# TensorE multiplies the identity matrix into an unread bank around the transposes of the RMS norms

## The reference

```
def rmsnorm(x, g):                       # first block; the second adds shift and scale
    y = x * rsqrt(mean(x * x, axis=-1) + 1e-6)
    return y * g
first block, for l in 0, 1:
    h = rmsnorm(x, norm_mix_g[l]);  proj = h @ w_in[l]      # attention, retention, gates
    x = x + (gated branches) @ w_out[l]
    h = rmsnorm(x, norm_mlp_g[l]);  x = x + square(relu(h @ w_up[l])) @ w_down[l]
second block, for l in 0, 1:
    hn = modulate(rms_norm(h, norm_g[l, 0]), sh1, sc1);  h = h + 0.5 * g1 * swiglu(hn, ffn1)
    hn = modulate(rms_norm(h, norm_g[l, 1]), sh2, sc2);  h = h + g2 * (mixed(hn @ w_in[l]) @ w_out[l])
    hn = modulate(rms_norm(h, norm_g[l, 2]), sh3, sc3);  h = h + 0.5 * g3 * swiglu(hn, ffn2)
```

## Time and profile before

| | us |
|---|---|
| median of three runs | 2333.89 |
| lowest, highest run | 2333.36, 2339.49 |
| the profiled execution, its own time | 2334.86 |
| its span, first to last instruction | 2333.0 |
| PE busy (share of the span) | 2161.5 (93%) |
| DVE busy | 1447.8 (62%) |
| ACT busy | 1092.7 (47%) |
| mean granted TensorE clock | 0.95 |

### The profile page before, as it was taken

The page is one execution under the profiler, slowest core; times in us unless marked ns, Lnnn a source line. Parts: engine busy times, 40 slices in busy tenths (PEclk is TensorE's granted clock), DMA queues, the critical chain, the costliest instruction groups (busy, mean ns, idle before and its releaser), DMA issues.

```text
span 2333.0 us, 34753 instructions
## 1 busy us (share of the span) xinstructions
PE 2161.5 (93%) x13908; PEld 1931.7 (83%) x13908; DVE 1447.8 (62%) x1914; ACT 1092.7 (47%) x1738; POOL 57.9 (2%) x40
## 2 busy tenths in 40 slices
PE   6999989999889998999789989799988998989998
PEld 6878878998869887899779978689977997868997
DVE  4455646888435654888765565765556556576555
ACT  4236724433424752543445544555544554355554
POOL 0110000000001000000010000000001000000000
PEclk9999999999889999999889999999999999988999
DMA  6343236987424225788544532135544453323553
GB/s 230 111 163 109 91 137 254 366 353 298 157 80 181 94 76 196 293 355 352 219 158 171 191 133 106 73 127 181 181 160 152 175 188 137 109 73 111 180 191 115
DMA packets 55606, 409.71 MB, mean 176 GB/s; under 512 B 6544, under 2 KB 6800, under 8 KB 7184
## 3 DMA queue, kind: packets, MB, share of 16 engines
q1 hardware_dynamic: 45936, 330.20, 38.8%
q10 hardware_dynamic: 9504, 77.21, 8.4%
HBM read 406.34 MB, written 1.05 MB: 175 GB/s over the span
## 4 chain that ended last, share of the span: by engine, by line
PE 82%; DVE 10%; ACT 5%; issue 3%; DMA 1%; DVEq 0%; POOLq 0%; ACTq 0%; SPq 0%
PE bank L490 23%; PE bank L491 22%; PE bank L492 22%; PE bank L904 4%; DVE weights_low L335 1%; DVE work L1338 1%; ACT weights_high L325 1%; DVE weights_low L337 1%; PE bank L980 1%; PE bank L1558 1%; PE bank L794 1%; PE bank L753 1%; DMA raw_weights<-in_stream 1%; ACT scratch L396 1%; PE bank L774 1%
## 5 line engine op out<-in xcount | busy, mean ns | idle before, releaser
L490 PE MATMUL bank<-h_high,weights_high 128*128 128x256 f32 x2944 | 858.1, 291 | 32.7 <-DVE h_low L465 26.9
L491 PE MATMUL bank<-h_low,weights_high 128*128 128x256 f32 x2944 | 844.6, 287 | 0.0
L492 PE MATMUL bank<-h_high,weights_low 128*128 128x256 f32 x2944 | 844.0, 287 | 0.0
L325 ACT ACTIVATE weights_high<-raw_weights 128x1024 fp32r<-128x1024 f32 x292 | 309.1, 1059 | 847.9 <-PE bank L492 748.3
L335 DVE TENSOR_TENSOR weights_low<-raw_weights,weights_high 128x1024 fp32r<-128x1024 f32 x292 | 361.1, 1237 | 499.3 <-ACT weights_high L325 497.1
L490 PEld LDWEIGHTS bank<-h_high,weights_high 128*128 128x128 f32 x2944 | 576.6, 196 | 55.1 <-issue 46.9
L491 PEld LDWEIGHTS bank<-h_low,weights_high 128*128 128x128 f32 x2944 | 577.2, 196 | 3.5 <-issue 1.9
L492 PEld LDWEIGHTS bank<-h_high,weights_low 128*128 128x128 f32 x2944 | 576.5, 196 | 0.0
L337 DVE TENSOR_TENSOR weights_low<-raw_weights,weights_high 128x1024 fp32r<-128x1024 f32 x292 | 359.3, 1231 | 0.0
L326 ACT ACTIVATE weights_high<-raw_weights 128x1024 fp32r<-128x1024 f32 x292 | 305.2, 1045 | 0.0
L490 PE MATMUL bank<-weights_high,hidden_high 128*128 128x512 f32 x608 | 239.4, 394 | 12.5 <-DVE hidden_low L592 12.5
(11 more groups left out here) (274 smaller groups left out, 2168.2 us busy)
## 6 DMA issues: line engine op xcount, KB each, us to landing
raw_weights<-in_stream SPq DMA_DIRECT2D x310, 1024.0 KB, 4.8
work<-in_ada ACTq DMA_DIRECT2D x64, 1152.0 KB, 9.4
consts<-in_consts SPq DMA_DIRECT2D x1, 2112.0 KB, 9.7
work<-in_row ACTq DMA_DIRECT2D x2, 836.0 KB, 4.6
x<-in_x SPq DMA_DIRECT2D x1, 1024.0 KB, 5.0
out_x<-x SPq DMA_DIRECT2D x1, 1024.0 KB, 3.9
gain_row<-in_final SPq DMA_DIRECT2D x1, 512.0 KB, 9.8
vec<-in_vec SPq DMA_DIRECT2D x1, 169.0 KB, 9.3
```

Source lines behind the costliest of these rows:

```text
L325: act.activation(high[:, 0:SPLIT], raw[:, 0:SPLIT], ACT.Copy).then_inc(m["high_a"], 1)
L490: pe.matmul(out, aH, bH, start=start, stop=False, skip_group_check=True)
L491: pe.matmul(out, aH, bL, start=False, stop=False, skip_group_check=True)
L492: return pe.matmul(out, aL, bH, start=False, stop=stop, skip_group_check=True)
```

## The change

`pe_norm` gets an argument `spare` and calls a new function `pe_keep`, which multiplies the 128x128 identity (plain float32) by itself into the first 128 columns of a bank that nobody reads then. All four `pe_begin` move to the front. Where `s` is a number, eight such matmuls stand ahead of the transposes of tt 0 and two between tt 0 and tt 1. Seven stand behind the last transpose in every call. They carry no semaphore. The bank is `m.ps[6]`, save for the eight ahead of "n2" of the second block, where bank 6 is still being read and the norm's own first bank is used, which the transposes then overwrite.

```diff
-def pe_norm(pe, m, plan, s, name):
+def pe_norm(pe, m, plan, s, name, spare=None):
+    for b in range(4):
+        pe_begin(pe, m, plan, f"{name}_{b}")
+    if s is not None:
+        pe_keep(pe, m.bank(plan, f"{name}_0") if spare is None else spare, m.const("ident"), 8)
     for tt in range(2):
+        if tt == 1 and s is not None:
+            pe_keep(pe, m.ps[6], m.const("ident"), 2)
         for b in range(4):
-            if tt == 0:
-                pe_begin(pe, m, plan, f"{name}_{b}")
             if s is not None and b % 2 == 0:
                 pe.wait_ge(m["xn_ready"], 4 * s + 2 * tt + b // 2 + 1)
...
             if tt == 1:
                 mm.then_inc(m.bank_full[plan.group[f"{name}_{b}"] % 4], 1)
+    pe_keep(pe, m.ps[6], m.const("ident"), 7)
+
+def pe_keep(pe, bank, ident, n):
+    for _ in range(n):
+        pe.matmul(bank[:, 0:P], ident, ident, start=True, stop=True)
...
-    pe_norm(pe, m, plan, 0, "n2")
+    pe_norm(pe, m, plan, 0, "n2", m.ps[6])
...
-    pe_norm(pe, m, plan, 1, "n3")
+    pe_norm(pe, m, plan, 1, "n3", m.ps[6])
```

## The result

| | before | after |
|---|---|---|
| median of the runs, us | 2333.62 (2330.97 to 2339.49, 8 runs) | 2343.32 (2336.87 to 2347.74, 8 runs) |
| profiled execution, us | 2334.86 | 2342.15 |
| span, us | 2333.0 | 2340.3 |

The ratio is 1.0041, with a 95% interval of 1.0025 to 1.0056: slower by about 9.7 us, where 2332.6 was forecast. That lies above the range (2325.5 to 2342).

The account below looks back on a forecast made before the run. PE was taken to bound the kernel (82% of the chain), with clock lost behind the norms. 2.6 - 1.9 - 2.0 + 0 = -1.3 us gave 2333.6 profiled, median 2332.6 us, range 2325.5 to 2342.

Parts of the forecast that it names:

- The price of an added matmul, 0.22 us: On PE at full clock each added identity matmul costs 0.22 us: eight 1.75, two 0.44, seven 1.53.
- n2 of the first block, +1.3 each: Transposes delayed by the eight, no clock gain; 1.3 us lost in each of two executions, +2.6 us.
- The room under the wait: First block's n2: 0.40 us between PE's possible start at 373.68 and the transposes at 374.08; the eight need 1.75.
- n2 of the second block, -1.1 and -0.8: Added matmuls hidden; full clock behind the norm wins 1.1 us in layer 0, 0.8 in layer 1, -1.9 us.
- n3, -0.85 and -1.15: Second block's n3: 1.05 us delay against 1.9 and 2.2 us won behind it in layers 0 and 1, -2.0 us.
- n1, 0: Only the seven are added; first block between +1.9 and about -0.6 each, taken as 0; second block hidden, 0.
- The rule against it: Transposes don't count as clock-gate activity like matmuls; mostly-transpose norms would fall to half clock anyway, giving 2351 us.
- The second rival: Clock ignores the added matmuls and falls in the second block's norms as before; losses sum to 17.6 us, 2351; chance 0.10.
- The sum: Norm terms 2.6 - 1.9 - 2.0 + 0 give -1.3 us for the whole kernel; forecast's chance 0.58.
- The fourth rival: Half-clock stretches elsewhere in the kernel move too, either sign, some 5 to 8 us; chance 0.09.

Follow-up runs that it names:

- a2: Changed kernel without the eight and two matmuls ahead of and between the transposes, keeping the seven behind them; 1.0008 of the kernel before.
- a0: The changed kernel run again, unedited, for a second trace; 2343.03 us, 1.0051 of the kernel before.
- c1: Kernel before with the second block's 48 four-column matmuls (group ff) widened to 128 columns; 0.9954 of the kernel before.
- c2: Changed kernel with the second block's 48 four-column matmuls (group ff) widened to 128 columns; 0.9977 of the kernel before.
- a1: Changed kernel without the seven matmuls behind the transposes, keeping the eight and two; 1.0038 of the kernel before.
- g3: Kernel before with three idle 0.7 us DVE additions ahead of the second block's n2, both layers; its trace loses 3.9 us from 1370 us on.
- g4: Kernel before with four idle 0.7 us DVE additions ahead of the second block's n2, both layers; its median and ratio aren't in the text.
- c3: Kernel before with group ff widened to 128 columns and the one-column modulation matmuls to 96; 0.9905 of the kernel before.
- e2: Changed kernel with group ff widened to 128 columns and the one-column modulation matmuls to 96; 0.9917 of the kernel before.
- a3: Changed kernel with the eight and two only in the second block's n2, the seven everywhere; 2337.82 us, 1.0017 of the kernel before.
- e1: Changed kernel with the eight into the spare bank moved ahead of the waits for the norm banks; 1.0006 of the kernel before.
- e3: Kernel before with ff and modulation widened, added matmuls only in n2 and n3, the leading ones ahead of the waits; 2309.77 us, 0.9890.
- g1 to g4: Kernel before with one, two, three or four idle 0.7 us DVE additions ahead of the second block's n2; two cost more than three.
- b0_copy: The kernel before run again, unedited, one execution for a second trace; 2333.08 us.

## Why the prediction was wrong

- **The price of an added matmul, 0.22 us: right.** Two records each; the eight hold PE for 1.86 us, where 1.75 was forecast.
- **n2 of the first block, +1.3 each: right** (+1.37, +1.36). The room under the wait was as small as worked out.
- **n2 of the second block, -1.1 and -0.8: right** (-1.14, -1.05).
- **n3, -0.85 and -1.15: right** (-0.83, -0.99), and a2 measured the gross gain without the delay, 1.97 and 2.11 against 1.9 and 2.2. What the forecast missed is how little the head did for it: without the eight and the two the gain is the same to 0.3 us.
- **n1, 0: right** (-0.15 up to 372 us and -0.4 over layer 1's n1, against the repeated kernel). The 1.4 us that the first trace of before has more is a difference between two executions of one kernel.
- **The rule against it** (the Trainium skill, "TensorE: Matmul & The Clock Gate", Part 4, on transposes). In the first block's n2 the clock stood at 1.00 in every trace, with or without added matmuls. In the second block it fell within or just behind the transposes of n2 and n3 in the kernel before, and behind the norm it was 1.00 wherever seven plain matmuls followed them. PE had idled ahead of those transposes, and no run separates the idling from the transposes, so the rule isn't refuted there. The second rival is refuted: with the added matmuls the clock was 1.00 behind all four of these norms.
- **The sum: wrong.** -1.3 us holds for the norms (-1.28) and not for the kernel (+9.0 in the trace, +9.7 in the medians). The step that failed is the one that sets the half-clock stretches elsewhere to zero. The fourth rival named them, "either sign, some 5 to 8 us", at 0.09; it is what happened. By this pair of traces they came to +10.25 us, of which the 5.65 of s3 and s4 came again in a0, and 4.3 of the 9.7 us went when the narrow matmuls of s3 and s4 were widened (c1, c2).

What could have been read before: the profile shows 29 half-clock stretches, 234 us in all, and seven of the eight groups of one-column matmuls end in one. I looked at the stretches behind the norms alone. A kernel whose clock falls in so many places has no place "elsewhere" whose cost may be taken as nothing when what lies ahead of it moves. And the first trace of before had the first group without a fall, and in layer 0 the last of the 48 matmuls of four columns had begun when the clock fell: s1 and s3 were about as short as in any trace with the narrow matmuls, so that a move there could hardly win (s4 could win: 24.7 in a1, g3 and g4, against 27.07).

What stays open: how much of the 4.6 us at s1, s2 and 828 us is due to the change and how much to the one execution; what makes the half of the last 3 us between c3 and e2 that doesn't lie at the norms; why the step at 828 us, behind a wait of 1.7 us on PE, comes in some traces and not in others (after, a0, a3, c2, e1 and e3 have it, the other twelve don't); why executions of g1 to g4 entered the first block's fall when b0_copy didn't. No version was found in which the change's steps fall at the old places.

## What to carry to other kernels

Before costing a change on a kernel with a granted clock below 1, list its half-clock stretches and what PE ran ahead of each; if many stand behind narrow matmuls, widen those first (it was free here and gave 22 us), and treat any local sum of a few us as uncertain by the price of one or two such stretches. Fill-in matmuls behind a wait delayed the path here, ahead of it they nearly didn't; the ones behind the transposes, with nothing to wait for them, did the work. Test head and tail apart. A repeated trace of the kernel before is worth one run: it shows which differences come without any edit.

## What the runs showed of the hardware

- Records of matmuls of 1, 4, 96 and 128 columns, each with a fresh weight tile, all start 0.11 us apart at full clock. In the first trace of before the narrow ones were followed by half clock, or met it, in 7 of 8 groups and in both layers' ff; in c3, where they are wide, in none (two falls come later, in PE's waits).
- A half-clock stretch of 3.4 us in matmuls costs 1.5 us (s1: 12.05 to 13.53). One of 17.07 us that begins among the 48 narrow matmuls goes with 7.2 us more than in the kernel with wide ones, which has none there (s3: 22.69 to 29.90).
- Stretch lengths come in steps: s3 was 22.7, 25.9, 27.6, 28.3 or 29.9 us in 18 traces, s4 21.5, 24.7, 27.1 or 28.7.
- The traces of after and a0_copy, 2.3 us apart at 372 us and 5.1 at 830, show the same steps from there on; so do the two traces of the kernel before, 1.8 us apart. It looks as if a kernel fell into step with the moments at which the clock changes. This is argued from those four traces and not tested by itself.
- Seven plain float32 matmuls (14 records of 0.11 us) between a norm's last transpose and the next product went with clock 1.00 behind it in 32 of 32 cases, against 5 of 40 without them.
